# Feed-forward up steps: the low product ahead of the high one for every row block

## The chip, the cores and the metric

The kernel runs on one core of a Trainium2 chip. The metric is the device time of one execution in microseconds; the time before is the median of three runs. TensorE (PE in the profile) multiplies matrices: a weight load (PEld) puts a 128x128 block into the array, and a matmul streams columns past it and adds its results up in a bank of PSUM. VectorE (DVE), ScalarE (ACT), GpSimd (POOL) and the DMA queue of SyncE (SP) work beside it, and semaphores order them.

## What is computed

The reference is a chain of two small transformers on 256 tokens of width 1024. Six times in it stands a gated feed-forward block, two in the first model and four in the second. This is the part that the change touches:

```python
FFN_HIDDEN = D_FF = 2816

def swiglu(hn, w_in, w_out):
    gate, up = jnp.split(hn @ w_in, 2, axis=-1)
    return (jax.nn.silu(gate) * up) @ w_out

# in each model, six times in all (FFN_RES_WEIGHT only in the second)
x = x + swiglu(rmsnorm(x, g), w_in, w_out)
```

Everything is fp32, and the kernel reaches that accuracy by splitting each operand into a high part and a low rest.

## The kernel before, in words

**Tiles.** The weights come in tiles of 128x2048 values, one DMA of SP each, into `raw`. ScalarE makes the high part `whi` of a tile and VectorE the low part `wlo = raw - whi`. There are three slots of each. A semaphore for each (`hi_made`, `lo_made`) tells TensorE that a tile is split; `tile_split` waits for both.

**The activations** stand transposed in `ysp`, 128 partitions by 2 parts by 8 row blocks by 256 tokens. Part 0 is the high part and is also called `yh`, part 1 is the low part `yl`. A row block is 128 of the 1024 input features; the matmuls of one result add up over eight of them (`k` from 0 to 7).

**An up step** (`up` inside `ffn`) makes 128 hidden units: their gate and their up column, for all 256 tokens. It uses one tile. Its two column blocks (`c` = 0 is the gate, `c` = 1 the up product) go to a PSUM bank each; the pairs of banks 6, 7 and 0, 1 alternate from step to step. For each row block there are two matmuls on the bank. The *high* product has the high weights `hi` as its stationary block and streams both parts of the activations, 512 columns, into both halves of the bank (line 1068). The *low* product has the low weights `lo` and streams `yh` alone, 256 columns, into the first half (line 1067, or 1070 in row block 0). VectorE later adds the two halves. So a block has 8 high and 8 low matmuls, a step 16 and 16.

**Order.** The order on TensorE is the order of the code. `bank_free` waits until VectorE and ScalarE have read the bank out. Each of the six feed-forward blocks begins with a pair of steps that is made otherwise (`token_pair`). Then come two single up steps, each behind two small transposes (`hidden_turn`, line 1052), then one down step. After that come nine *pairs*: two up steps back to back (`ups`), then a down step (`down`). Eight of these pairs run in a hardware loop (`Fori`), the ninth behind it. A down step is a long row of matmuls of 512 columns (lines 856 to 858, in `three`). So 6 x (2 + 18) = 120 up steps go through `up`, of which 108 stand in 54 pairs, and 12 behind transposes.

**Readers of an up step.** VectorE's `tensor_reduce` (lines 2262 and 2263) and ScalarE's silu (line 1669) work behind `step_done`, which the last matmul of a step sets.

Of the kernel before, what the change touches and what calls it, by code (L numbers as in the profile page):

```python
# [25 lines left out]
P = 128  # L26
# [293 lines left out]
def build(nc, stream, side, xin, misc, dilb, second, gains, mlag, small, rows, gate_rows, out):  # L320
    ctx = ExitStack()
    with ctx:
# [6 lines left out]
        def at(name, off, cols, dt=F32, shape=None):  # L329

            t = nc.alloc_sbuf_tensor_at(name, [P, cols], dt, offset=base[0] + off)
            a = t[:, :]
            if shape:
                names = "abcdef"[:len(shape)]
                a = a.rearrange(f"p ({' '.join(names)}) -> p {' '.join(names)}", **dict(zip(names, shape)))
            return a
# [8 lines left out]
        ysp = at("ysp", 88 * K, 2 * KC * S, F32R, (2, KC, S))  # L345
        yh, yl = ysp[:, 0], ysp[:, 1]
# [248 lines left out]
        def rows3(t, kc, w):  # L595
            return t[:, 0:kc * w].rearrange("p (k n) -> p k n", k=kc)

        def bank2(i):
            return pb[i].rearrange("p (a n) -> p a n", a=2)
# [253 lines left out]
        def _(pe):  # L853
            def three(o, a, b, first, last):

                pe.matmul(o, a[1], b[0], start=first, stop=False)  # L856
                pe.matmul(o, a[0], b[1], start=False, stop=False)  # L857
                return pe.matmul(o, a[0], b[0], start=False, stop=last)  # L858

            def tile_split(B, tile):  # L860
                n = B.tile_no(tile) + 1
                pe.wait_ge(hi_made, n)
                pe.wait_ge(lo_made, n)

            def bank_free(B, step, first):

                for s, who in ((drain_act, "A"), (drain_dve, "D")):
                    n = B.drained(step if first else step - 1, who)
                    if type(n) is not int or n > 0:
                        pe.wait_ge(s, n)  # L870
# [65 lines left out]
            def norm_late(B, stage, n):  # L936

                tb = B.plan.tb[stage]
                return {(0, 0): lambda who: copied_by(B, tb + 1, who), (0, 4): lambda who: copied_by(B, tb + 2, who),
                        (0, 6): lambda: turn(B, stage, n, 1, 0), (0, 7): lambda: turn(B, stage, n, 1, 1),  # L940
                        (1, 0): lambda: copied(B, tb + 3), (1, 4): lambda: copied(B, tb + 4)}
# [25 lines left out]
            def token_pair(B, stage, i, tile, beside=False, late={}):  # L967

                step = B.plan.step[stage] + i
                for m in range(M):  # L970
                    if m == 0 or not beside:
                        bank_free(B, step + m, beside)
                    if m == 0 and late:
                        first_half(B, stage, tile, late)
                        continue
                    t = slice(m * P, m * P + P)
                    for k in range(KC):
                        if m == 0 and k % 4 == 0:
                            tile_split(B, tile + k // 4)
                        s = B.slot(tile + k // 4)  # L980
                        hi, lo = side_of(stage)[0::2] if beside and k >= 4 else (whi[s], wlo[s])
                        c = slice(512 * (k % 4), 512 * (k % 4) + 512)
                        if (m, k) in late:
                            late[(m, k)]()
                        last = three(pb[m], (yh[:, k, t], yl[:, k, t]), (hi[:, c], lo[:, c]), k == 0, k == KC - 1)
                        if m == 1 and k % 4 == 3:
                            last.then_inc(step_done, 1)
                    if m == 0:
                        last.then_inc(row_done, 1)
# [53 lines left out]
            def ffn(B, stage, f, norm_stage, n, then=None, turn_last=False):  # L1043

                t0, s0 = B.plan.tile[stage], B.plan.step[stage]
                up_banks = ((6, 7), (0, 1))

                def hidden_turn(m):

                    pe.wait_ge(drain_dve, B.drained(s0 + m + 1, "D"))  # L1050
                    for c in range(2):
                        last = pe.transpose(pb[4 + m][:, c * P:c * P + P], h32[m][:, c * P:c * P + P], ident)
                    last.then_inc(ht_done, 1)

                def up(B, step, bank):

                    tile = t0 + step - 1
                    tile_split(B, tile)
                    bank_free(B, s0 + step, False)
                    s = B.slot(tile)  # L1060
                    hi, lo = rows3(whi[s], 8, 256), rows3(wlo[s], 8, 256)
                    for c in range(2):
                        o = bank2(up_banks[bank][c])
                        for k in range(8):
                            cols = slice(c * P, c * P + P)
                            if k:
                                pe.matmul(o[:, 0, :], lo[:, k, cols], yh[:, k, :], start=False, stop=False, skip_group_check=True)  # L1067
                            last = pe.matmul(o, hi[:, k, cols], ysp[:, :, k, :], start=k == 0, stop=k == 7)  # L1068
                            if k == 0:
                                pe.matmul(o[:, 0, :], lo[:, k, cols], yh[:, k, :], start=False, stop=False, skip_group_check=True)  # L1070
                    last.then_inc(step_done, 1)

                def down_part(B, i, tile, j, k):

                    s = B.slot(t0 + tile)
                    hi, lo = rows3(whi[s], 2, 1024), rows3(wlo[s], 2, 1024)
                    t, c = slice(j // 2 * P, j // 2 * P + P), slice(j % 2 * 512, j % 2 * 512 + 512)
                    return three(pb[2 + j], (hh[i % 2][:, k, t], hl[i % 2][:, k, t]), (hi[:, k, c], lo[:, k, c]),
                                 i == 0 and k == 0, i == NF // 2 - 1 and k == 1)

                def down_ready(B, chunks, i, tile):

                    tile_split(B, t0 + tile)
                    pe.wait_ge(h_ready, chunks + 2 * i + 2)

                def down(B, chunks, i, tile):

                    down_ready(B, chunks, i, tile)
                    for j in range(4):
                        for k in range(2):  # L1090
                            last = down_part(B, i, tile, j, k)
                    last.then_inc(step_done, 1)

                def ups(B, i):
                    up(B, 3 * i - 1, 0)
                    up(B, 3 * i, 1)

                def pair(B, chunks, i):
                    ups(B, i)
                    down(B, chunks, i - 1, 3 * i)  # L1100

                token_pair(B, stage, 0, t0, True, norm_late(B, norm_stage, n))
                hidden_turn(0)
                up(B, 2, 0)
                hidden_turn(1)
                up(B, 3, 1)
                down(B, NF * f, 0, 3)
                with nc.tensor.Fori(0, FFN_ROUNDS) as r:
                    for i in (2, 3):
                        pair(B.later(r), NF * f + 4 * r, i)  # L1110
                last_i = NF // 2 - 1
                ups(B, last_i)
                down_ready(B, NF * f, last_i - 1, FFN_TILES - 2)
                for i, j in ((last_i - 1, 0), (last_i - 1, 1), (last_i - 1, 2), (last_i, 0), (last_i, 1), (last_i, 2), (last_i - 1, 3), (last_i, 3)):
                    if (i, j) == (last_i, 0):
                        down_ready(B, NF * f, last_i, FFN_TILES - 1)
                    for k in range(2):
                        if then and not turn_last and (i, j, k) == (last_i, 3, 1):
                            turn(*then, 0, 0)
                        last = down_part(B, i, FFN_TILES - 1 if i == last_i else FFN_TILES - 2, j, k)  # L1120
                    if j == 3:
                        last.then_inc(step_done, 1)
                    elif i == last_i:
                        last.then_inc(acc_done, 1)
                if turn_last:
                    turn(*then, 0, 0)
                if then:
                    turn(*then, 0, 1)
# [1863 lines left out]
```

## Time and profile before

| | |
|---|---|
| median of three runs | 1881.88 us (1881.71 to 1881.93) |
| the profiled execution, its own time | 1882.02 us |
| its span in the trace | 1880.2 us |
| TensorE matmul busy | 1863.6 us (99%), 10664 matmuls |
| weight loads busy | 1601.1 us (85%) |
| VectorE busy | 1340.4 us (71%) |
| ScalarE busy | 861.0 us (46%) |
| GpSimd busy | 124.3 us (7%) |

A matmul's duration in the trace reaches from its start to the arrival of its last result, and the next matmul starts long before that. Busy time of TensorE therefore says that it rarely stood still, not how fast it went. The speed is read from starts: from the start of one matmul to that of the next. Times on the trace's axis are microseconds from the span's start.

### The profile page before, as it was taken

The page shows a single profiled execution, that of the slowest core. Times are in us where ns is not written, and L with a number is a line of the kernel's source. Part 1 is how long each engine was busy: PE and PEld are TensorE (multiplying, and loading weights), DVE is VectorE, ACT ScalarE, POOL GpSimd, SP SyncE. Part 2 cuts the span into 40 slices and gives each one's busy share as a digit, 9 for nine tenths or more (in the row PEclk, how much of TensorE's full clock was granted, in tenths as well). Part 3 has the DMA queues.
Part 4 walks back from the last instruction along what each step waited for, and adds up shares of the span by engine and source line. Part 5 has one row for each costly group of instructions (what it writes and reads, how often), then busy time and mean ns, then how long its engine had stood idle before and what let it go on. Part 6 is the DMA issues. An engine that isn't in the chain of part 4 may idle for free.

```text
span 1880.2 us, 28201 instructions
## 1 busy us (share of the span) xinstructions
PE 1863.6 (99%) x10664; PEld 1601.1 (85%) x10664; DVE 1340.4 (71%) x1697; ACT 861.0 (46%) x1107; POOL 124.3 (7%) x155
## 2 busy tenths in 40 slices
PE   9999999999999999999999999999999999999998
PEld 8998888888888888888977888888888897788887
DVE  5676767776767776776876677677777767677777
ACT  5554434474334444344375433443335337644333
POOL 1001200230000100000300100010000020000000
PEclk9999999999999999999999999999999999999999
DMA  7423555425555565544434465556554444455453
GB/s 307 180 90 148 199 181 187 171 82 203 212 191 188 224 223 200 181 167 169 178 137 162 175 227 184 201 218 229 197 182 175 164 166 168 147 189 213 180 199 113
DMA packets 48548, 343.46 MB, mean 183 GB/s; under 512 B 5472, under 2 KB 5504, under 8 KB 8784
## 3 DMA queue, kind: packets, MB, share of 16 engines
q1 hardware_dynamic: 43200, 310.92, 45.5%
q0 software_dynamic: 5264, 31.35, 4.4%
q8 instruction: 61, 1.00, 0.2%
q14 instruction: 23, 0.19, 0.0%
HBM read 341.20 MB, written 1.05 MB: 182 GB/s over the span
## 4 chain that ended last, share of the span: by engine, by line
PE 66%; issue 0%; DVE 0%; POOL 0%; ACT 0%; DVEq 0%; POOLq 0%
PE bank L1068 16%; PE bank L856 12%; PE bank L858 12%; PE bank L857 12%; PE bank L1067 7%; PE bank L919 2%; PE bank L1070 1%; PE bank L1147 1%; PE bank L1519 1%; PE bank L964 1%; PE bank L959 1%; PE bank L960 1%; PE bank L1443 0%; PE bank L1381 0%; PE bank L1508 0%
## 5 line engine op out<-in xcount | busy, mean ns | idle before, releaser
L2065 DVE TENSOR_TENSOR wlo<-raw,whi 128x2048 fp32r<-128x2048 f32 x292 | 672.1, 2304 | 223.2 <-ACT whi L1586 222.7
L1586 ACT ACTIVATE whi<-raw 128x2048 fp32r<-128x2048 f32 x293 | 559.3, 1910 | 256.4 <-PE bank L858 252.3
L1068 PE MATMUL bank<-ysp,whi 128*128 128x512 f32 x1920 | 666.1, 396 | 0.0
L1067 PE MATMUL bank<-ysp,wlo 128*128 128x256 f32 x1680 | 468.6, 279 | 0.0
L1068 PEld LDWEIGHTS bank<-ysp,whi 128*128 128x128 f32 x1920 | 347.7, 188 | 67.0
L1067 PEld LDWEIGHTS bank<-ysp,wlo 128*128 128x128 f32 x1680 | 316.8, 189 | 10.7
L1669 ACT ACTIVATE sg<-sg 128x256 f32<-128x256 f32 x120 | 50.2, 418 | 468.2 <-DVE sg L2262 468.2
L856 PE MATMUL bank<-whi,ysp 128*128 128x512 f32 (+3 forms) x592 | 217.3, 367 | 0.3 <-DVE wlo L2065 0.3
L858 PE MATMUL bank<-whi,ysp 128*128 128x512 f32 (+3 forms) x592 | 212.8, 359 | 0.0
L857 PE MATMUL bank<-wlo,ysp 128*128 128x512 f32 (+3 forms) x592 | 212.4, 359 | 0.0
L856 PE MATMUL bank<-whi,hl 128*128 128x512 f32 x528 | 206.0, 390 | 0.0
L858 PE MATMUL bank<-whi,hh 128*128 128x512 f32 x528 | 205.5, 389 | 0.0
L857 PE MATMUL bank<-wlo,hh 128*128 128x512 f32 x528 | 205.5, 389 | 0.0
L2262 DVE TENSOR_REDUCE sg<-bank 128x256 f32<-128x512 f32 x120 | 82.9, 691 | 88.7 <-PE bank L1068 88.7
L856 PEld LDWEIGHTS bank<-whi,ysp 128*128 128x128 f32 x592 | 111.7, 189 | 23.3 <-issue 6.7
L858 PEld LDWEIGHTS bank<-whi,ysp 128*128 128x128 f32 x592 | 111.7, 189 | 16.9
L857 PEld LDWEIGHTS bank<-wlo,ysp 128*128 128x128 f32 x592 | 111.9, 189 | 15.2
L858 PEld LDWEIGHTS bank<-whi,hh 128*128 128x128 f32 x528 | 99.1, 188 | 20.9
L857 PEld LDWEIGHTS bank<-wlo,hh 128*128 128x128 f32 x528 | 99.2, 188 | 20.8
L856 PEld LDWEIGHTS bank<-whi,hl 128*128 128x128 f32 x528 | 99.1, 188 | 18.0
L707 POOL TENSOR_TENSOR rstd<-ms,half 128x1 f32<-128x1 f32 (+3 forms) x29 | 19.1, 660 | 1353.7 <-DVE ms L2110 993.4
L856 PE MATMUL bank<-ysp,wlo 128*128 128x256 f32 x320 | 91.5, 286 | 0.0
(359 smaller groups left out, 2356.7 us busy)
## 6 DMA issues: line engine op xcount, KB each, us to landing
raw<-stream SPq DMA_DIRECT2D x294, 1024.0 KB, 4.8
sr<-side POOLq DMA_DIRECT2D x10, 1024.0 KB, 5.2
gbc<-gains POOLq DMA_DIRECT2D x11, 512.0 KB, 3.9
cw<-small POOLq DMA_DIRECT2D x2, 2048.0 KB, 10.7
gbias<-gate_rows POOLq DMA_DIRECT2D x6, 512.0 KB, 4.3
dbias<-dilb POOLq DMA_DIRECT2D x1, 2304.0 KB, 12.8
lng<-rows POOLq DMA_DIRECT2D x2, 1024.0 KB, 5.2
tab<-second POOLq DMA_DIRECT2D x1, 1724.0 KB, 15.0
```

The source lines that it names most:

```text
L707: pool.tensor_tensor(dst[:, c], src[:, c], e[:, c], ALU.pow).then_inc(rstd_ready, 1)
L856: pe.matmul(o, a[1], b[0], start=first, stop=False)
L857: pe.matmul(o, a[0], b[1], start=False, stop=False)
L858: return pe.matmul(o, a[0], b[0], start=False, stop=last)
L919: last = pe.transpose(o[0:rows, i * P:i * P + P], b, ident)
L959: pe.matmul(pb[0], yh[:, 4 * q + k, t], lo[:, c], start=q == 0 and k == 0, stop=False)
L1067: pe.matmul(o[:, 0, :], lo[:, k, cols], yh[:, k, :], start=False, stop=False, skip_group_check=True)
L1068: last = pe.matmul(o, hi[:, k, cols], ysp[:, :, k, :], start=k == 0, stop=k == 7)
L1586: act.activation(whi[s], raw[s], ACT.Copy).then_inc(hi_made, 1)
L1669: act.activation(sg[j % 2], sg[j % 2], ACT.Silu).then_inc(silu_done, 1)
L2065: dve.tensor_tensor(wlo[s], raw[s], whi[s].bitcast(F32), ALU.subtract).then_inc(lo_made, 1)
L2262: dve.tensor_reduce(sg[j % 2], gate.rearrange("p a n -> p n a"), AX_X, ALU.add).then_inc(gate_made, 1)
```

## The change

The low product now stands ahead of the high one in row block 0 as well, as it already does in the seven others. The first matmul on the bank is then a low one, and it has the `start` flag; the high matmul of row block 0 comes second, without that flag. The same matmuls are made, as many as before, with the same operands and waits, and nothing changes on other engines.

```diff
@@ -1060,14 +1060,10 @@
                     s = B.slot(tile)
                     hi, lo = rows3(whi[s], 8, 256), rows3(wlo[s], 8, 256)
                     for c in range(2):
-                        o = bank2(up_banks[bank][c])
+                        o, cols = bank2(up_banks[bank][c]), slice(c * P, c * P + P)
                         for k in range(8):
-                            cols = slice(c * P, c * P + P)
-                            if k:
-                                pe.matmul(o[:, 0, :], lo[:, k, cols], yh[:, k, :], start=False, stop=False, skip_group_check=True)
-                            last = pe.matmul(o, hi[:, k, cols], ysp[:, :, k, :], start=k == 0, stop=k == 7)
-                            if k == 0:
-                                pe.matmul(o[:, 0, :], lo[:, k, cols], yh[:, k, :], start=False, stop=False, skip_group_check=True)
+                            pe.matmul(o[:, 0, :], lo[:, k, cols], yh[:, k, :], start=k == 0, stop=False, skip_group_check=True)
+                            last = pe.matmul(o, hi[:, k, cols], ysp[:, :, k, :], start=False, stop=k == 7, skip_group_check=True)
                     last.then_inc(step_done, 1)
```

TensorE, where the loop's first up step begins behind the last matmul of a down step (line 858), before. `whi` and `wlo` are the weights' parts, `ysp` the activations; 128x512 is a high product, 128x256 a low one.

```order
L858 MATMUL bank<-whi_52,hh_138 128x512
L1108 UNCONDITIONAL_BRANCH
L1108 ISA
L870 ISA
L1068 MATMUL bank<-ysp,whi_53 128x512
L1070 MATMUL bank<-ysp,wlo_56 128x256
L1067 MATMUL bank<-ysp,wlo_56 128x256
L1068 MATMUL bank<-ysp,whi_53 128x512
```

The same place now.

```order
L858 MATMUL bank<-whi_52,hh_138 128x512
L1104 UNCONDITIONAL_BRANCH
L1104 ISA
L870 ISA
L1065 MATMUL bank<-ysp,wlo_56 128x256
L1066 MATMUL bank<-ysp,whi_53 128x512
L1065 MATMUL bank<-ysp,wlo_56 128x256
L1066 MATMUL bank<-ysp,whi_53 128x512
```

High, low, low, high has become low, high, low, high.

TensorE, inside the same step, from the last low matmul of column block 0 into column block 1, before:

```order
L1067 MATMUL bank<-ysp,wlo_56 128x256
L1068 MATMUL bank<-ysp,whi_53 128x512 x2
L1070 MATMUL bank<-ysp,wlo_56 128x256
L1067 MATMUL bank<-ysp,wlo_56 128x256
L1068 MATMUL bank<-ysp,whi_53 128x512
```

And now:

```order
L1065 MATMUL bank<-ysp,wlo_56 128x256
L1066 MATMUL bank<-ysp,whi_53 128x512
L1065 MATMUL bank<-ysp,wlo_56 128x256
L1066 MATMUL bank<-ysp,whi_53 128x512
L1065 MATMUL bank<-ysp,wlo_56 128x256
L1066 MATMUL bank<-ysp,whi_53 128x512
```

Two high matmuls in a row, and then two low ones, stood at each edge between column blocks. Now low and high alternate strictly through both blocks, and through both steps of a pair.

## Rows read from the trace of the kernel before

**Rows 1.** The page: span, busy times, and the chain that ended last by line.

```profile
span 1880.2 us, 28201 instructions
PE 1863.6 (99%) x10664; PEld 1601.1 (85%) x10664; DVE 1340.4 (71%) x1697; ACT 861.0 (46%) x1107; POOL 124.3 (7%) x155
PE bank L1068 16%; PE bank L856 12%; PE bank L858 12%; PE bank L857 12%; PE bank L1067 7%; PE bank L919 2%; PE bank L1070 1%; PE bank L1147 1%; PE bank L1519 1%; PE bank L964 1%; PE bank L959 1%; PE bank L960 1%; PE bank L1443 0%; PE bank L1381 0%; PE bank L1508 0%
```

**Rows 2.** Waits of TensorE: us in total, times, longest; first and tenth row.

```profile
PE bank L919 <- DVE y L2120: 2.7, 2, 1.5
...
PE bank L856 <- DVE wlo L2065: 0.3, 1, 0.3
```

**Rows 3.** Matmuls of the up steps, whole run: duration in ns, min/median/max.

```profile
L1068 PE MATMUL bank<-ysp,whi x1920: 389/395/481, 176.2 to 1862.3; 128*128 128x512 f32 x192
...
L1067 PE MATMUL bank<-ysp,wlo x1680: 274/280/285, 176.7 to 1862.1; 128*128 128x256 f32 x187
...
L1070 PE MATMUL bank<-ysp,wlo x240: 277/277/285, 176.6 to 1860.0; 128*128 128x256 f32 x120
```

**Rows 4.** Windows: the four column blocks of one pair (PE, PEld, DVE, ACT, POOL; clock).

```profile
209.85:212.66 2.81, 2.81 (x18) 2.45 (x16) 0.69 (x2) 1.92 (x1) 0.00 (x0) 1.00 0.54 146
212.66:215.44 2.78, 2.78 (x18) 2.43 (x17) 1.63 (x1) 0.00 (x0) 0.00 (x0) 1.00 0.55 230
215.44:218.25 2.81, 2.81 (x17) 2.45 (x16) 2.37 (x5) 1.89 (x2) 0.00 (x0) 1.00 0.93 321
218.25:221.03 2.78, 2.78 (x18) 2.42 (x16) 2.36 (x2) 0.34 (x1) 0.00 (x0) 1.00 0.13 53
```

**Rows 5.** Timeline of TensorE, first column block: start us, duration us, matmul.

```profile
209.85 0.39 PE L1068 MATMUL bank<-ysp,whi 128*128 128x512 f32 x1
210.07 0.28 PE L1070 MATMUL bank<-ysp,wlo 128*128 128x256 f32 x1
210.19 0.28 PE L1067 MATMUL bank<-ysp,wlo 128*128 128x256 f32 x1
210.31 0.40 PE L1068 MATMUL bank<-ysp,whi 128*128 128x512 f32 x1
210.54 0.28 PE L1067 MATMUL bank<-ysp,wlo 128*128 128x256 f32 x1
...
211.60 0.28 PE L1067 MATMUL bank<-ysp,wlo 128*128 128x256 f32 x1
...
212.31 0.28 PE L1067 MATMUL bank<-ysp,wlo 128*128 128x256 f32 x1
212.43 0.63 PE L1068 MATMUL bank<-ysp,whi 128*128 128x512 f32 x2
```

**Rows 6.** Timeline of TensorE, second column block: low matmuls of row blocks 1 and 7.

```profile
213.01 0.27 PE L1067 MATMUL bank<-ysp,wlo 128*128 128x256 f32 x1
...
215.09 0.27 PE L1067 MATMUL bank<-ysp,wlo 128*128 128x256 f32 x1
```

**Rows 7.** Durations in these two blocks, ns, min/median/max; first and last start.

```profile
L1070 PE MATMUL bank<-ysp,wlo x1: 278/278/278, 210.1 to 210.1; 128*128 128x256 f32 x1
...
L1067 PE MATMUL bank<-ysp,wlo x1: 278/278/278, 211.3 to 211.3; 128*128 128x256 f32 x1
...
L1067 PE MATMUL bank<-ysp,wlo x6: 278/281/284, 210.5 to 212.3; 128*128 128x256 f32 x6
...
L1067 PE MATMUL bank<-ysp,wlo x7: 274/274/280, 213.0 to 215.1; 128*128 128x256 f32 x7
...
L1068 PE MATMUL bank<-ysp,whi x7: 395/398/403, 210.3 to 212.4; 128*128 128x512 f32 x7
```

**Rows 8.** A single up step behind transposes: timeline row, then windows of its two blocks.

```profile
182.07 0.48 PE L1068 MATMUL bank<-ysp,whi 128*128 128x512 f32 x1
...
182.07:184.94 2.87, 2.87 (x19) 2.52 (x18) 2.45 (x5) 1.07 (x2) 2.77 (x10) 1.00 1.01 380
184.94:187.76 2.82, 2.82 (x18) 2.45 (x16) 2.43 (x4) 1.16 (x1) 2.82 (x5) 1.00 0.54 221
```

## The prediction

> **What bounds the kernel now.** I began with the page [rows 1]. TensorE's matmuls are busy for 1863.6 us of a span of 1880.2, and VectorE, next among the other engines, for 71%. The chain that ended last runs almost wholly over matmul lines, and the lines of the up steps (1068, 1067, 1070) are 24% of the span in it. Then I read the waits of TensorE [rows 2]. The longest group is 2.7 us in total, at a norm's transposes, and the wait for a split tile is 0.3 us, once. So no other engine or transfer holds the up steps up, and the kernel's time is the sum of the distances between starts of matmuls. A change can only pay or cost here if it changes such distances. The clock shows as 1.00 in every window [rows 4], which is the 2.4 GHz level.
>
> A busy TensorE hides how fast it goes, so the next views are windows and a timeline with starts. One pair of up steps is four column blocks with the same 8 high and 8 low matmuls each. They don't take the same time [rows 4]: 2.81, 2.78, 2.81 and 2.78 us, 11.18 together. TensorE is busy throughout in all four, and what VectorE, ScalarE and the DMAs do beside them differs without a pattern (VectorE 0.69 and 2.37 us in the two long ones).
>
> The timeline shows what differs. In the first block, after its opening, three pairs of low and high take from 210.54 to 211.60, 1.06 us, or 0.353 a pair [rows 5]. In the second block six pairs take from 213.01 to 215.09, 2.08 us, or 0.347 a pair [rows 6]. The durations show two rhythms as well [rows 7]. In the long block the low matmuls last 278, 281 or 284 ns and the high ones up to 403. In the short one the low matmuls last 274 or 280. I call them the **slow rhythm** (it repeats after three pairs, 1.06 us) and the **fast rhythm** (two pairs, 0.693 us). Both have the same operands in shape, so the rhythm is a state that TensorE carries from one matmul to the next. The blocks alternate between the two, and what stands between them is exactly what the change removes: high, high, low, low at the block's edge.
>
> **The change, part by part.** No instruction, byte or wait is added or removed. What moves is one low matmul for each of 240 column blocks [rows 3], past one high matmul.
>
> The opening itself. High, low, low, high of row blocks 0 and 1 take from 209.85 to 210.54, 0.69 us for two pairs [rows 5]. That is the price of two pairs in the fast rhythm (0.693), so the irregular opening costs nothing by itself. Its removal gains nothing directly. What it does is choose the rhythm for the rest of the block: behind 512-column matmuls or a fast block the slow one follows, behind a slow block the fast one [rows 4].
>
> The new order has no such place in a pair of steps. 64 matmuls alternate strictly from the first low one on, and a rhythm that is steady inside a block should last over all four. The question is which rhythm the entry sets. The first low matmul behind the 512-column ones lasts 278 ns [rows 7], and the next starts 0.12 us behind it [rows 5]. In the slow rhythm one low matmul of each three is also 278 ns (that at 211.3), in the fast one none is; there it is 274 or 280. Behind the 278 ns one a high matmul follows in the slow rhythm, and that is also what the new order puts behind the entry. I conclude that the new order enters the slow rhythm at that point and stays in it.
>
> The pairs of steps. 32 pairs in the slow rhythm are ten periods of 1.06 and two pairs more, of 0.35 and 0.35 to 0.36: 11.30 to 11.31 us. Before it was 11.18. The loss is 0.12 to 0.13 us; I take 0.122, since the entry starts with the period's short pair. Times 54 pairs of steps this is **+6.6 us**.
>
> The exit. The last high matmul is followed by the 512-column ones of the down step. At the phase where 32 pairs end, it is one that lasts 403 ns, while the period's shortest is 395 [rows 7]. Bounds: nothing, and 8 ns times 54, 0.4 us. I take half, **+0.2 us**.
>
> The single steps. Twelve steps stand behind two transposes. One takes 2.87 + 2.82 = 5.69 us [rows 8], 0.10 over 5.59 in the loop, and its first matmul lasts 0.48 us, not 0.39: it waits at the entry, and the changed one will too. The trace of before doesn't show a low matmul behind a transpose, so I bound it. All slow, the step is 16 x 0.353 + 0.09 = 5.74, which is +0.6 us over twelve. All fast, it is 16 x 0.347 + 0.09 = 5.64, which is -0.6. The slow one is the likelier as in the loop, but the entry is another one: **+0.2 us**.
>
> The `start` flag moves from a high matmul of 512 columns to a low one of 256. The flagged high matmul at 209.85 lasts 0.39 us and the next starts 0.22 behind it, no more than any unflagged high one [rows 5]. I give it nothing; were it 1 ns either way, 240 times would be 0.24 us.
>
> On the other engines nothing moves. A slower up step gives VectorE and ScalarE more room, and TensorE waits for them so little [rows 2] that this gives nothing back: less than 0.3 us.
>
> Sum: 6.6 + 0.2 + 0.2 = +7.0 us on 1882.02 of the profiled execution, 1889.0. The median of the runs is 0.14 below that execution, so the forecast is **1888.9 us**, 0.37% slower.
>
> **The rivals.**
>
> *No memory that matters: the order is free.* If each block's time is the sum of its matmuls, whatever their order, nothing changes: 1881.9. For it speaks that the opening costs just two fast pairs. Against it stand the 0.03 us between blocks of equal content, four times in four [rows 4]. Here too belongs that the strict order falls into each rhythm for about half of the blocks, for instance since a wait at the edge of a step sets it anew; that is 54 x (16 x 0.3533 + 16 x 0.3467 - 11.18), or +1 us.
> The Trainium skill ("TensorE: Matmul & The Clock Gate", sections "Back-to-back issue gap" and "LDWEIGHTS (loading the stationary operand)") gives N / 2.4 + 2.5 ns for a matmul of N columns and 106.7 ns for the load of 128. By that an estimate for a pair is 109 + 216 = 325 ns in any order, no load shows anywhere, and the change is worth nothing. This case's trace has 347 and 353 ns for a pair, so some 22 to 28 ns are outside that rule, and it is these that change.
>
> *The fast rhythm.* This is the case on the other side. If the entry's 278 ns is not the slow rhythm's state but one that leads into the fast one, all four blocks run at 0.347 a pair: 32 x 0.3467 = 11.09 us, -0.086 for each of 54, -4.6 us, and up to -0.6 from the single steps: 1882.02 - 0.14 - 5.2 = 1876.7. For it speaks that two low matmuls in a row are gone, and that the low matmul behind the two high ones of 212.43 [rows 5] leads into the fast rhythm [rows 6]. Against it, that low matmul is followed by a low one too, and the entry behind the down step, as it stands in the trace, has always led into the slow one. It decides from the point where the third low matmul of a pair of steps lasts 274 or 280 and not 284 ns.
>
> *Chances.* Slow rhythm 0.70, order free or a mixture 0.17, fast rhythm 0.13. This measurement can tell about 0.2%, 3.8 us, from no change. The slow rhythm's own range is 1886.5 to 1890.3: below, part of the blocks escape it, and above it gets all of the bounds (6.9 + 0.4 + 0.6 + 0.2 us on 1881.9, 1890.0) and a little. The range for 8 in 10 takes in the free order: **1881.5 to 1890.3**. It leaves out the fast rhythm and little else. Faster 0.13, same 0.16, slower 0.71.
>
> **What the changed kernel's profile would show.** In a pair of steps all four windows take 2.82 to 2.83 us and together 11.30; the low matmuls last 278, 281 and 284 ns in turn from the first to the last, and no 274 is among them in the loop. The median duration of the low matmuls rises from 280 to 281, and the lowest high one lasts 395. I am wrong in the step on the entry if low matmuls of 274 fill the loop, and in the step that a rhythm lasts if the windows of one pair still differ by 0.03 us. The down steps (512 columns throughout), the count of matmuls and TensorE's waits stay as they are.

## The result and the profile after

The changed kernel takes 1890.67 us (median of 5 runs, 1890.61 to 1891.11), the kernel before beside it 1881.76. The ratio is 1.0049, 95% interval 1.0038 to 1.006: 0.5% slower. The profiled executions take 1890.67 and 1882.02 us, a difference of 8.65. The prediction had the direction and the place right, and 7.0 where 8.65 was to be explained; 1890.67 lies 0.4 us above its range.

The page of the changed kernel, against [rows 1]. VectorE and ScalarE do what they did, and TensorE is busy for 8.5 us more with the same 10664 matmuls.

```profile
span 1888.9 us, 28201 instructions
PE 1872.1 (99%) x10664; PEld 1603.5 (85%) x10664; DVE 1339.9 (71%) x1697; ACT 860.8 (46%) x1107; POOL 124.4 (7%) x155
```

The windows of the four column blocks of the same pair of up steps as in [rows 4]. Columns are the window, its length, then busy us and instructions of PE, PEld, DVE, ACT and POOL. The fifth window is the start of the down step behind the pair, twelve distances between matmuls of 512 columns.

```profile
209.87:212.69 2.82, 2.82 (x17) 2.45 (x16) 0.68 (x1) 1.92 (x1) 0.00 (x0) 1.00 0.50 145
212.69:215.52 2.83, 2.83 (x18) 2.46 (x17) 1.62 (x1) 0.00 (x0) 0.00 (x0) 1.00 0.61 234
215.52:218.35 2.83, 2.83 (x18) 2.45 (x16) 2.39 (x5) 1.91 (x2) 0.00 (x0) 1.00 0.86 316
218.35:221.17 2.82, 2.82 (x17) 2.45 (x16) 2.33 (x2) 0.32 (x1) 0.00 (x0) 1.00 0.11 47
221.17:223.94 2.77, 2.77 (x13) 2.25 (x12) 2.32 (x5) 1.84 (x2) 0.00 (x0) 1.00 0.62 148
```

The reader is to see two things. All four blocks now take 2.82 or 2.83 us, together 11.30 where before had 11.18: no short block is left. And the twelve distances of the down step take 2.77 us. The same window of the kernel before, which the prediction did not look at:

```profile
221.03:223.75 2.72, 2.72 (x13) 2.25 (x12) 2.28 (x5) 1.80 (x2) 0.00 (x0) 1.00 0.50 154
```

The durations of the low matmuls in that pair of steps, and of single ones at its entry (ns, min/median/max, first and last start), against [rows 7]:

```profile
L1065 PE MATMUL bank<-ysp,wlo x32: 277/281/284, 209.9 to 220.8; 128*128 128x256 f32 x32
...
L1065 PE MATMUL bank<-ysp,wlo x1: 278/278/278, 209.9 to 209.9; 128*128 128x256 f32 x1
...
L1065 PE MATMUL bank<-ysp,wlo x1: 281/281/281, 210.2 to 210.2; 128*128 128x256 f32 x1
...
L1065 PE MATMUL bank<-ysp,wlo x1: 284/284/284, 210.6 to 210.6; 128*128 128x256 f32 x1
```

278, 281, 284 from the first low matmul on: the slow rhythm starts at the entry, and among all 32 none lasts 274. That decides against the fast rhythm and against the free order.

The timeline at the exit, high matmul of row block 7 and the first of the down step (start us, duration us):

```profile
220.93 0.40 PE L1066 MATMUL bank<-ysp,whi 128*128 128x512 f32 x1
221.17 0.40 PE L856 MATMUL bank<-whi,hl 128*128 128x512 f32 x1
221.41 0.40 PE L857 MATMUL bank<-wlo,hh 128*128 128x512 f32 x1
221.64 0.40 PE L858 MATMUL bank<-whi,hh 128*128 128x512 f32 x1
221.88 0.39 PE L856 MATMUL bank<-whi,hl 128*128 128x512 f32 x1
```

Distances of 0.24, 0.23 and 0.24 us stand where the settled row of such matmuls has 0.2267 (2.720 over twelve). The slow rhythm runs on into matmuls that are all of one length. By the trace's starts in ns, nine distances behind it are off the settled value, 0.049 us over in all, in each of the 54 down steps. The kernel before is 0.004 us over there, in one distance, so the difference is 0.045.

A single up step behind transposes, against [rows 8]:

```profile
181.90:184.80 2.90, 2.90 (x19) 2.54 (x18) 2.47 (x5) 1.10 (x2) 2.86 (x10) 1.00 0.90 322
184.80:187.64 2.84, 2.84 (x18) 2.46 (x17) 2.41 (x3) 1.12 (x1) 2.84 (x5) 1.00 0.67 280
```

It takes 5.74 us, before 5.69. Eleven of the twelve single steps take 5.73 or 5.74 us. One, with the same code, takes 5.64, and its low matmuls but the first last 280 ns:

```profile
457.10:462.74 5.64, 5.64 (x35) 4.95 (x34) 4.83 (x5) 2.19 (x2) 1.57 (x3) 1.00 0.98 403
```

So behind transposes the entry does not always set the same rhythm. Behind a down step it did, 54 times.

The account of the 8.65 us, from the starts of matmuls: 54 pairs of steps at 0.122, 6.6; the down steps behind them at 0.045, 2.4; the twelve single steps, 0.5; and 0.9 gained back elsewhere.

### The profile page after: what moved, and what is told of

Same layout as the page of the kernel before. It is cut to its first block, busy times and chain, and to the rows that moved or that the text cites. A ratio compares the mean times of both kernels' runs of the same rounds, so it can differ in the third digit from the quotient of the medians.

```text
span 1888.9 us, 28201 instructions
## 1 busy us (share of the span) xinstructions
PE 1872.1 (99%) x10664; PEld 1603.5 (85%) x10664; DVE 1339.9 (71%) x1697; ACT 860.8 (46%) x1107; POOL 124.4 (7%) x155
## 4 chain that ended last, share of the span: by engine, by line
PE 66%; issue 0%; DVE 0%; POOL 0%; ACT 0%; DVEq 0%; POOLq 0%
PE bank L1066 16%; PE bank L856 12%; PE bank L858 12%; PE bank L857 12%; PE bank L1065 8%; PE bank L919 2%; PE bank L1143 1%; PE bank L1515 1%; PE bank L964 1%; PE bank L959 1%; PE bank L960 1%; PE bank L1439 0%; PE bank L1377 0%; PE bank L1504 0%; PE bank L1384 0%
## 5 line engine op out<-in xcount | busy, mean ns | idle before, releaser
L1066 PE MATMUL bank<-ysp,whi 128*128 128x512 f32 x1920 | 681.3, 399 | 0.0
L1065 PE MATMUL bank<-ysp,wlo 128*128 128x256 f32 x1920 | 540.1, 281 | 0.0
L1066 PEld LDWEIGHTS bank<-ysp,whi 128*128 128x128 f32 x1920 | 360.8, 188 | 88.7
L1065 PEld LDWEIGHTS bank<-ysp,wlo 128*128 128x128 f32 x1920 | 362.6, 189 | 2.1
L856 PE MATMUL bank<-ysp,wlo 128*128 128x256 f32 x320 | 91.4, 286 | 0.0
```

Source lines behind the costliest of these rows:

```text
L1065: pe.matmul(o[:, 0, :], lo[:, k, cols], yh[:, k, :], start=k == 0, stop=False, skip_group_check=True)
L1066: last = pe.matmul(o, hi[:, k, cols], ysp[:, :, k, :], start=False, stop=k == 7, skip_group_check=True)
```

## The experiments

All orders are written by one loop in `up`, in place of the lines of the change:

```python
for c in range(2):
    o = bank2(up_banks[bank][c])
    order = [(low, k) for k in range(8) for low in (1, 0)]
    ...
    for n, (low, k) in enumerate(order):   # start flag on n == 0
```

As it stands this is the change's order. A *kink* is a place high, high, low, low in the row. It *flips* if the rhythm behind it is another than the one in front. The *exit* is the first twelve distances of the down step behind a pair. `bank` is 0 in the first step of a pair and 1 in the second. Some expectations count time in cycles of 1.2 GHz, 0.833 ns each: 416 of them are 0.3467 us.

### Kink at the edge inside each step

```diff
+    if c == 1:
+        order[0:2] = order[1::-1]
```

> Both steps of a pair: low product first in column block 0 (as in the change), high product first in column block 1 (as before). Rhythm theory (a high, high, low, low place flips the rhythm, strict alternation keeps it): the four blocks of a pair run slow, fast, fast, slow, about 2.82, 2.78, 2.78, 2.82 us, so the up steps take what they took before, and what follows a slow exit (0.044 us in the down step behind it, 54 times) may stay: 1882 to 1884.5 us. Rival (each low-first opening has its own price, wherever it stands, the start flag on the short matmul for instance): half of the 240 openings, half of the change's 8.9 us, 1886.2 us, and all blocks with the same order take the same time.

Measured: 1883.53 us, ratio 1.0009 (1.0 to 1.0018). Its four blocks and the exit:

```profile
209.98:212.81 2.83, 2.83 (x18) 2.45 (x16) 0.70 (x2) 1.92 (x1) 0.00 (x0) 1.00 0.40 151
212.81:215.59 2.78, 2.78 (x17) 2.43 (x16) 1.62 (x1) 0.00 (x0) 0.00 (x0) 1.00 0.53 224
215.59:218.37 2.78, 2.78 (x18) 2.43 (x16) 2.33 (x5) 1.85 (x2) 0.00 (x0) 1.00 0.92 324
218.37:221.18 2.81, 2.81 (x17) 2.45 (x16) 2.39 (x2) 0.38 (x1) 0.00 (x0) 1.00 0.13 52
221.18:223.92 2.74, 2.74 (x13) 2.25 (x12) 2.29 (x5) 1.81 (x2) 0.00 (x0) 1.00 0.56 146
```

Slow, fast, fast, slow. The first and the third block have the same order and differ by 0.05 us; the price for each low-first opening is out. The 1.7 us over before are the exit (2.74 against 2.72) and the blocks (11.20 against 11.18), 0.9 us each over 54.

### Kink at the edge between steps and at the entry

```diff
+    if c == 0:
+        order[0:2] = order[1::-1]
```

> The other way round: high product first in column block 0, low product first in column block 1. Rhythm theory: the entry sets the slow rhythm, it lasts through block 1, the next step's opening flips it: slow, slow, fast, fast, about 2.82, 2.82, 2.78, 2.78 us, with a fast exit: 1881 to 1883 us. Rival (a price for each low-first opening): 1886.2 us, as for the run before it.

Measured: 1887.8 us, ratio 1.0031 (1.0019 to 1.0043). A miss, and not the rival's number either.

```profile
210.08:212.89 2.81, 2.81 (x17) 2.45 (x16) 0.70 (x2) 1.92 (x1) 0.00 (x0) 1.00 0.51 152
212.89:215.73 2.84, 2.84 (x18) 2.45 (x16) 1.63 (x1) 0.00 (x0) 0.00 (x0) 1.00 0.60 228
215.73:218.54 2.81, 2.81 (x18) 2.45 (x16) 2.37 (x5) 1.89 (x2) 0.00 (x0) 1.00 0.98 321
218.54:221.37 2.83, 2.83 (x17) 2.46 (x16) 2.36 (x2) 0.33 (x1) 0.00 (x0) 1.00 0.11 43
221.37:224.09 2.72, 2.72 (x13) 2.25 (x12) 2.27 (x5) 1.79 (x2) 0.00 (x0) 1.00 0.51 163
```

The kink in front of the third block did not flip the rhythm. My theory, that a kink always flips, is wrong. All four blocks are slow, 11.29 us against 11.18, and 54 x 0.11 = 5.9 us are the whole difference. For though the last block is slow, this exit costs nothing, 2.72.

What differs is the place in the slow rhythm's period. Its high matmuls last 395, 403 and 398 ns in turn. The last two high ones in front of the kink (the first and last start, ns min/median/max), in this kernel, which doesn't flip:

```profile
L1072 PE MATMUL bank<-ysp,whi x2: 398/400/403, 215.1 to 215.5; 128*128 128x512 f32 x2
```

In the kernel before, and in the one with the kink inside each step, which flip:

```profile
L1068 PE MATMUL bank<-ysp,whi x2: 395/396/398, 212.1 to 212.4; 128*128 128x512 f32 x2
```

```profile
L1072 PE MATMUL bank<-ysp,whi x2: 395/399/403, 212.2 to 212.6; 128*128 128x512 f32 x2
```

By the turn of the three, 403 and then 398 stand up to the kink here (the second is its first matmul), 398 and then 395 in the kernel before, 395 and then 403 in the other.

### One kink early, one kink late

```diff
+    if (bank, c) == (0, 1):
+        order[0:2] = order[1::-1]
```

> Low product first everywhere but in column block 1 of the first step of a pair (60 of 240 blocks open with the high product). Rhythm theory: slow, then fast for the three blocks that follow, and a fast exit: one slow block less than before for each of 54 pairs, 54 x 0.037 = 2.0 us under before, 1879.5 us. Rival (a price for each low-first opening): three quarters of 8.9 us over before, 1888.4 us.

Measured: 1880.51 us, ratio 0.9992 (0.9983 to 1.0001). Blocks of 2.82, 2.79, 2.77 and 2.78 us; slow, then fast three times, as expected, and 1.4 us under before where 2.0 were expected. 60 blocks open as before and 180 as in the change, so the rival's 1888.4 is far off.

```diff
+    if (bank, c) == (1, 1):
+        order[0:2] = order[1::-1]
```

> Low product first everywhere but in column block 1 of the second step of a pair. Rhythm theory: slow, slow, slow, fast, one slow block more than before, +2 us, and the exit is fast, so the down step behind it gives the 2.4 us of the change back: 1884 us. Rival (a price for each low-first opening): 1888.4 us, the same as with the kink early.

Measured: 1888.89 us, ratio 1.0037 (1.0024 to 1.005), a miss. The number is near the rival's, but the run with one kink early, for which the rival says the same, is 8.4 us away. The two high matmuls in front of the kink, and the timeline at it:

```profile
L1072 PE MATMUL bank<-ysp,whi x2: 398/400/403, 217.8 to 218.1; 128*128 128x512 f32 x2
...
218.14 0.62 PE L1072 MATMUL bank<-ysp,whi 128*128 128x512 f32 x2
218.60 0.40 PE L1070 MATMUL bank<-ysp,wlo 128*128 128x256 f32 x2
218.83 0.40 PE L1072 MATMUL bank<-ysp,whi 128*128 128x512 f32 x1
```

The kink stands at the place of the period where it failed in the run with the kink in block 0, and fails again: the block behind it is slow (218.38 to 221.19, 2.81 us). The two high matmuls that meet at it last 0.62 us together, where those of the kernel before last 0.63 [rows 5]. So of the three places in the period two flip and one doesn't, and the kernel's edge does not decide: a kink at this same edge flips in the kernel before.

### The kink at the entry

If the place decides, a kink behind the first pair of a pair of steps stands where the kernel before has it, behind a 395 ns matmul:

```diff
+    if (bank, c) == (0, 0):
+        order[2:4] = order[3:1:-1]
```

> Low product first in every block, but in the first block of a pair of steps the two products of row block 1 change places, so the order is low, high, high, low, low, high, and strictly alternating from there. Refined rhythm theory (a high, high, low, low place flips the slow rhythm into the fast one behind the period's 395 ns high matmul, as at each edge in the kernel before): 415 cycles of 1.2 GHz for the first pair, 836 for the next two, and 29 fast pairs of 416.5: 11.11 us for a pair of steps where before took 11.18, 54 x 0.075 = 4.0 us under before, 1877.9 us, and no slow block in the loop. Rival (the flip needs a settled slow rhythm, and so close to the entry it doesn't come): all four blocks slow, 1890 us. Rival (price for each low-first opening): 1890.7 us.

Measured: 1878.22 us, ratio 0.9981 (0.9972 to 0.999).

```profile
209.49:212.27 2.78, 2.78 (x17) 2.42 (x16) 0.64 (x2) 1.92 (x1) 0.00 (x0) 1.00 0.50 144
212.27:215.05 2.78, 2.78 (x18) 2.43 (x17) 1.66 (x1) 0.00 (x0) 0.00 (x0) 1.00 0.55 233
215.05:217.82 2.77, 2.77 (x18) 2.42 (x16) 2.33 (x5) 1.85 (x2) 0.00 (x0) 1.00 0.92 322
217.82:220.59 2.77, 2.77 (x17) 2.42 (x16) 2.39 (x2) 0.37 (x1) 0.00 (x0) 1.00 0.14 56
220.59:223.33 2.74, 2.74 (x13) 2.25 (x12) 2.30 (x5) 1.81 (x2) 0.00 (x0) 1.00 0.60 149
```

No block is slow. One pair of matmuls exchanged, 60 times in a kernel of 10664, is 12 us against the change, although all 240 blocks open with a low product and its `start` flag. Blocks two to four take 2.77 us, eight pairs at 0.3467, with such an opening each. So neither the flag nor the opening costs anything that shows; the rhythm does.

### The kink one pair later

```diff
+    if (bank, c) == (0, 0):
+        order[4:6] = order[5:3:-1]
```

> As the kink at the entry, but row block 2 and not 1 has its products exchanged: low, high, low, high, low, high, high, low, low, high. The kink then comes behind the period's 403 ns high matmul. Refined rhythm theory: it flips too (as in the run with the kink in block 1 alone), one slow pair more costs 0.02 us for a pair of steps, +1.0 us, and the fast rhythm then ends in its other half, where the exit costs 0.004 and not 0.023 us, -1.0 us: 1878.2 us, the same as with the kink a pair earlier. If the kink there leads back to the slow rhythm: 1890 us.

Measured: 1877.67 us, ratio 0.9979 (0.997 to 0.9988): the fastest version, faster than both kernels. It flips. Blocks of 2.79, 2.78, 2.77 and 2.77 us, and the exit window is 2.73 us where the kink a pair earlier has 2.74. In the traces the up steps take 0.018 us more for each pair of steps and the exit 0.018 us less, which cancels as expected. Of the 0.55 us between the two medians, 0.4 stand in the twelve single steps of the traces, where nothing was forecast.

### The two halves of the kink apart

```diff
-    order = [(low, k) for k in range(8) for low in (1, 0)]
+    order = [(low, k) for k in range(8) for low in ((1, 0) if c == 0 else (0, 1))]
```

> Column block 0 runs low, high in each row block, column block 1 runs high, low. So two high matmuls meet at the edge inside a step, and two low ones at the edge to the next step: the two halves of the kink stand apart. If the two high ones in a row flip the rhythm: slow, fast, then what the two low ones do (fast if they do nothing): 1878.5 to 1881 us. If it takes both together: slow throughout, 1889 to 1891 us. If the two low ones flip it: slow, slow, fast, fast and 1882 to 1884 us.

Measured: 1885.89 us, ratio 1.0021 (1.0012 to 1.0031), none of the three numbers.

The blocks from the second on, and the exit; the first is slow, 2.83 us:

```profile
212.63:215.41 2.78, 2.78 (x18) 2.44 (x16) 1.61 (x1) 0.00 (x0) 0.00 (x0) 1.00 0.52 218
215.41:218.19 2.78, 2.78 (x19) 2.43 (x17) 2.34 (x5) 1.85 (x2) 0.00 (x0) 1.00 1.02 330
218.19:221.00 2.81, 2.81 (x17) 2.45 (x16) 2.39 (x2) 0.37 (x1) 0.00 (x0) 1.00 0.11 47
221.00:223.78 2.78, 2.78 (x14) 2.26 (x13) 2.34 (x5) 1.85 (x2) 0.00 (x0) 1.00 0.49 194
...
L1068 PE MATMUL bank<-ysp,wlo x7: 280/280/281, 213.2 to 215.3; 128*128 128x256 f32 x7
```

Two high matmuls alone end the slow rhythm. They lead into a third one, in which every low matmul lasts 280 ns; it is as fast as the fast one (2.78). The two low ones lead from the third into the fast rhythm, at 2.78 us again. The next two high ones lead from the fast back into the slow, as in the kernel before. The exit window is the longest, 2.78 us, 0.06 over the settled row and 3.2 us over the kernel before in 54. It is no dearer kind of exit. By the starts in ns its first ten distances, from 0.241 and 0.238 us on, are within 0.5 ns those of the change from its last high matmul on. The down step's first matmul, 404 ns long in the pair shown, has taken the place of the period's 403 ns one, and its distance falls inside the window.

### Equal matmuls side by side

```diff
-    order = [(low, k) for k in range(8) for low in (1, 0)]
+    order = [(low, k) for low in (1, 0) for k in range(8)]
```

> Each block has its eight low products first and then its eight high ones. Rhythm theory: the loss is made where short and long matmuls meet out of step; rows of equal matmuls run at 144 cycles of 1.2 GHz for 256 columns and 272 for 512 wherever the trace of before has such rows, together 416 for a pair, as in the fast rhythm. So 32 x 416 = 13312 cycles, 11.09 us for a pair of steps, -0.09 us each, -4.8 us, if the eight changes of length cost nothing, and 1 to 2 us less gain if each costs some cycles: 1877 to 1879.5 us. Rival (the weight load behind a low matmul is exposed, so that a row of low ones is worse than alternation): each low-low distance would be longer than the 144 of other rows, and the time over 1882.

Measured: 1880.87 us, ratio 0.9995 (0.9986 to 1.0004). The gain is 1.0 us, less than expected. The windows of the first two blocks, and the timeline of the first:

```profile
209.63:212.42 2.79, 2.79 (x17) 2.46 (x16) 0.68 (x2) 1.92 (x1) 0.00 (x0) 1.00 0.50 138
212.42:215.22 2.80, 2.80 (x18) 2.46 (x16) 1.65 (x1) 0.00 (x0) 0.00 (x0) 1.00 0.56 237
...
209.63 1.12 PE L1068 MATMUL bank<-ysp,wlo 128*128 128x256 f32 x8
210.58 2.00 PE L1070 MATMUL bank<-ysp,whi 128*128 128x512 f32 x8
```

All blocks take alike, 2.79 or 2.80 us. Eight low matmuls take from 209.63 to 210.58, 0.95 us or 0.12 each, so a row of low ones is not slowed and the rival is out. Eight high matmuls take from 210.58 to 212.42, 1.84 us, where 8 x 0.2267 would be 1.81: the first five behind the low row are longer, as in an exit. The change from low to high costs 0.03 us, the one back gives 0.01, and so a block is 0.02 us over the fast rhythm's. Strict alternation in the fast rhythm, 2.77, is better than groups.

### Low products of full length

```diff
-    last = pe.matmul(o[:, 0, :], lo[:, k, cols], yh[:, k, :], ...)
+    last = pe.matmul(o, lo[:, k, cols], ysp[:, :, k, :], ...)
```

> The change's order, but the low product streams both parts of the activations, 512 columns, into the whole bank (the result gains the low times low product). All matmuls have then one length. Rhythm theory: no rhythm is left, all distances are 272 cycles (0.2267 us), 3.63 us for each block alike, 240 x (3.627 - 2.80) = +199 us: about 2080 us. If the rhythm came from the change of weights between high and low tiles, and not from the length, windows of the four blocks would still differ.

Measured in a single run: 2081.29 us. Windows of two blocks and of the exit:

```profile
216.35:219.98 3.63, 3.63 (x18) 3.00 (x16) 1.52 (x2) 1.92 (x1) 0.00 (x0) 1.00 0.62 212
219.98:223.60 3.62, 3.62 (x17) 3.00 (x16) 0.81 (x1) 0.00 (x0) 0.00 (x0) 1.00 0.65 188
...
230.86:233.58 2.72, 2.72 (x14) 2.25 (x12) 2.28 (x5) 1.80 (x2) 0.00 (x0) 1.00 0.85 355
```

16 x 0.2267 = 3.627 in each block, and no exit. With the same tiles, slots, banks and waits, no rhythm is left. Rows of short ones alone have none either (the run before this one), so it comes from the mixture of lengths.

### The exit by itself

The term that was wrong is taken alone: the changed kernel, its slow rhythm cut one or two pairs earlier. Both leave out part of the sum over features in a quarter of the blocks.

```diff
+    if (bank, c) == (1, 1):
+        order = order[:14]      # the second run: order[:12]
```

> The changed kernel, but the last block of each pair of steps leaves out row block 7 (one low and one high matmul, part of the sum over features), so the slow rhythm ends one pair earlier in its period, behind its 395 ns high matmul and not its 403 ns one. Exit theory (what the down step's first matmuls lose depends on the place in the period where the rhythm is cut): the nine first distances of the down step lose 0.02 us and not 0.045, so beside the work left out (54 x 0.358 + 6 x 0.354 = 21.5 us) it gains 1.5 us more: 1867.7 us. Rival (the exit costs the same wherever it comes): 1869.2 us.

> As the run before it, with row blocks 6 and 7 left out of that block: the rhythm is cut behind its 398 ns high matmul. Exit theory: nothing is lost behind it, as in the run with the high product first in block 0: beside the work left out (54 x 0.704 + 6 x 0.707 = 42.3 us) 2.6 us more: 1845.8 us. Rival (the same cost for every exit): 1848.4 us.

Measured: 1867.93 and 1846.15 us, 0.2 and 0.35 us from the exit theory, 1.3 and 2.25 from the rival. The exit windows, of the first run and of the second:

```profile
220.28:223.02 2.74, 2.74 (x13) 2.25 (x12) 2.47 (x6) 1.81 (x2) 0.00 (x0) 1.00 0.50 102
```

```profile
219.15:221.87 2.72, 2.72 (x13) 2.25 (x12) 2.48 (x6) 1.56 (x2) 0.00 (x0) 1.00 0.32 57
```

Over the settled row, behind the period's matmul of 403 ns the exit costs 0.049 us (the change), behind the one of 395 ns 0.021, behind the one of 398 ns nothing. That is how the expectation comes to 1.5 us; the 0.045 that it names is over the kernel before. The traces' starts show what differs: nine distances are off the settled value behind the 403 ns matmul, four behind the 395 ns one and none behind the 398 ns one.

## Why the prediction was right or wrong

**What bounds the kernel.** Right. TensorE's waits stayed as they were, but for 0.4 us at a norm, and the change's cost is all in distances between starts of the up steps and of the down steps behind them.

**The entry sets the slow rhythm.** Right. The first low matmul lasts 278 ns as forecast, and the kink at the entry alone, with everything else as in the change, takes 12 us off.

**It lasts over four blocks.** Right, in each of 54 pairs: 11.30 us against the 11.30 to 11.31 of the prediction, and 6.6 us against its term of 6.6.

**The start flag and the opening cost nothing.** Right; 240 flagged low openings stand in the two fastest versions.

**The single steps.** The term was +0.2 as a middle between bounds of 0.6 either way; 0.5 was measured, near the upper bound. Eleven are slow as in the loop and one is not, so that its caution about another entry was right. What decides there was not tested.

**The exit.** This is the step that failed. The prediction said: "Bounds: nothing, and 8 ns times 54, 0.4 us. I take half, **+0.2 us**." It measured 2.4 us. The list of what the profile would show has the same error: the down steps were to stay as they are. That a rhythm cut there costs something was right. The size was off by six times its upper bound, for the prediction had wrong how far the disturbance reaches. The 8 ns were the difference in duration of the last high matmul alone, as if the disturbance ended with it. The runs showed that it is handed on through nine matmuls of the down step and adds up to 0.045 us. The rest of my argument rests on a rhythm that lives on from one matmul to the next, and I did not apply it here. The trace of before has no exit behind the 403 ns matmul, but it has one out of a slow block, behind the single step of [rows 8], and I did not read it:

```profile
187.76:190.50 2.74, 2.74 (x13) 2.25 (x12) 2.60 (x5) 1.44 (x2) 2.74 (x8) 1.00 0.28 48
```

It is 0.02 us over the settled 2.72, spread over four distances. Times 54 that is 1.1 us, and it shows that one matmul's 8 ns are no upper bound.

**Given back elsewhere.** Put at less than 0.3 us, 0.9 were, and that offset more than a third of the exit's miss. I take it for luck and for nothing that the change does, since the rest of the kernel spreads as much among kernels that differ in the up steps alone. All but the up steps and the exits takes 1053.0 us before and 1052.1 after, and 1052.1 to 1053.1 in the thirteen traces. The largest piece is one distance, from a matmul of line 1190 to one of line 919: 0.53 us before and 0.11 after. Six of the traced kernels have 0.51 to 0.53 there and seven 0.11, and the two with the kink in the first block, one pair apart, have one each. At the start, seven distances at line 1202 are shorter after (five of them 0.11 us in place of 0.21), 0.6 us in all, and the wait at the norm behind them is 0.4 us longer, so 0.2 is left. What sets these was not tested.

**The flip.** The prediction's sentence that behind a slow block the kink leads to the fast rhythm is true for the kernel before, and not in general: it depends on the place in the period. The change has no kink, so this cost the forecast nothing, but two experiments were misjudged by it.

**The rivals.** The free order fell with the equal blocks of equal order that differ by 0.05 us, and the fast rhythm with the 278, 281, 284 ns.

What the inside of TensorE does in the three places of the period stays open. That the lengths must differ is shown; whether the weight load behind a short matmul is what comes late was not separated.

## What to carry to other kernels

Where TensorE is the bound and matmuls of two lengths alternate, measure distances between starts, block by block, before changing an order "at no cost": windows of equal work that differ by 1% and repeat are a state that the row of matmuls carries. One exchange of neighbours can set that state for sixty matmuls, for better (-0.2% here) or worse (+0.5%). And a disturbance doesn't end with the instruction that is changed: take its tail into the sum until the distances are back at their settled value.

## What the runs showed of the hardware that was not expected

- Rows of one mixture, 256 and 512 columns alternating at a granted clock of 1.00, have at least three steady rhythms: 2.82 or 2.83 us for 16 matmuls (durations 278, 281, 284 of the short ones), 2.77 (274, 280) and 2.78 (280 alone).
- Two long matmuls and then two short ones end the slow one at two of the three places of its period (395 and 403 ns, two kernels or more each) and not at the third (398 ns, two kernels). Two long ones alone ended it at the one place that was tried, 403 ns.
- Behind the slow rhythm a row of equal 512-column matmuls needs up to nine matmuls to settle, at a cost of nothing, 0.021 or 0.049 us over the settled row by the place where it is cut (398, 395 or 403 ns). The fast rhythm has an exit too: 0.004 us behind its 395 ns matmul and 0.023 behind its 392 ns one.
- Matmuls of one length have no rhythm once they have settled: 0.2267 us each for 512 columns, sixteen times over and in every block, and 0.12 us each for 256 in rows of eight. Their sum, 0.3467, is a pair of the fast rhythm; a pair of the slow one is 0.0067 over it.
